# A mixture-of-experts tail: gathering tokens in float32 from X, one more home for expert weights, and two filler products

## The chip, the cores and the metric

The kernel runs on one core of one Trainium2 chip. The metric is the time of one execution on the device in microseconds. TensorE multiplies, VectorE (DVE in the profile), ScalarE (ACT) and GpSimd (POOL) work on elements, and SyncE (SP) issues nearly all DMA transfers, which 16 DMA engines carry out. Weights come from the chip's main memory into on-chip memory of 128 partitions; products are summed in eight banks.

## The reference, cut to what matters

Two transformer blocks over 256 tokens of width 1024. The first has three kinds of attention and a convolutional feed-forward part, the second a gated linear attention, a pooling mixer, and a mixture of experts. The change lies in the last part, which computes:

```python
h2 = rmsnorm_2(x, norm2_g)                       # 256 tokens x 1024
g_p, g_idx = top_k(softmax(h2 @ w_rg + b_rg), 1) # one group of four
e_top, e_idx = top_k(expert logits inside that group, 2)
gate = g_p * softmax(e_top)                      # two weights for each token
# 32 experts; expert e takes the tokens that chose it:
y = (silu(xb @ w_gate[e]) * (xb @ w_up[e])) @ w_down[e]    # 1024 -> 256 -> 1024
x = x + sum over the two experts of gate * y
return rmsnorm_2(x, norm_f_g)
```

All values are float32. The weights of one expert are 3 MB, those of all 32 are 96 MB.

## The kernel before, in words

**Units and homes.** Weights come in units of 128 partitions x 2048 float32 (1 MB, rows of 8 KB). Up to `U_EXP` they run through a ring of six. The 96 units of the experts, three for each (two halves of the gate and up weights, then one of the down weights), go to 22 homes (`DEEP`) in turn: the six of the ring and 16 spaces whose first content is dead by then. `first_homes` lists them in the order of filling; `home_of(n)` gives the home of unit n, `loads_of(n)` how often that home has been loaded. SP issues everything on one queue, in the order of its program (lines 552 to 635). The first 22 units each wait until their home is free (lines 568 to 608): `LAST_1` and `LAST_2`, two homes in the arena, wait until the last unit before the experts is used; `FEATURES` waits for the router's product; `X_SLOT`, the space of X itself, waits until X has been squared, split and added. Each later unit waits until the unit 22 ahead of it has been used (lines 609 to 612). At the end SP loads the row of the final norm into X's space (line 614).

**Order of the work on TensorE** (lines 1240 to 1375): transposes of X, router, expert logits, the residual (X copied into four banks by products with the identity), one filler product (`stay_busy`), ranks of the tokens in their experts, then the gather, the first products of expert 0 and 1, the table of tokens and weights, and a loop over experts. In it come, for each expert: fold, down product, scatter of the expert ahead of it, and up products of the next; every fourth expert, the gather of the next four in two halves.

**Gather.** The tokens of an expert are at most 32 in the first pass (more are treated in a later loop). For four experts at once, the kernel multiplies X with a matrix of zeros and ones, `ONEHOT`. X is taken as two float32r parts: ScalarE copies a high part (`HNH`, lines 1768 and 1775), VectorE subtracts it from X for the low part (`low_part`, L2431 in the profile, four calls), and for each of 8 blocks of 128 features and each half of the tokens, TensorE multiplies the high and the low part with the float32r onehot (L1270): 32 products for a batch. A float32 product appears in the profile as two records, a float32r product as one.

**Around it.** VectorE chooses the experts between the logits and `m_ready` in some 25 dependent small steps, then forms ranks and the onehot, takes the gathered tokens out of the banks, and prepares the operands of the table (`table_in`). ScalarE squares X, and later scales, gates and weights results. VectorE and ScalarE make the weighted results of each expert in the space `YH` ("weighted"), at the place `FFN_FLOAT32` in the arena.

Of the kernel before, what the change touches and what calls it, by code (L numbers as in the profile page):

```python
# [68 lines left out]
DEEP, EARLY, SPARE = 22, 6, 2  # L69
# [14 lines left out]

LEFT = D // 2
# [41 lines left out]
def parts_before(event):  # L127
    return sum(NORM_PARTS[:event])
# [13 lines left out]

class Chain:
# [17 lines left out]
def build(nc, x_in, units_in, const_in, vec_in, rows_in, small_in, bias_in, out):  # L161
# [8 lines left out]
    with ctx:  # L170
# [28 lines left out]
        final_row = X[:, 0, :]  # L199
# [12 lines left out]
        with nc.sbuf_tensor("tokens_low_0", [P, D], f32r) as TOKENS_LOW_0:  # L212
            pass
# [28 lines left out]
        with ExitStack() as space:  # L242
            space.enter_context(nc.sbuf_tensor("ahead_of_parts", [P, PARTS_AT], fp32))
            HNH = space.enter_context(nc.sbuf_tensor("tokens_high", [P, TT, D], f32r))
            TOKENS_LOW_1 = space.enter_context(nc.sbuf_tensor("tokens_low_1", [P, D], f32r))
            ONEHOT = space.enter_context(nc.sbuf_tensor("batch_onehot", [P, TT, BATCH * CH], f32r))
        HNL = (TOKENS_LOW_0, TOKENS_LOW_1)

# [77 lines left out]
        x_space = flat(X[:, :, :])  # L326
# [67 lines left out]
        A.at = TT * D + D + TT * BATCH * CH  # L394
        XB = A.tile(KD, BATCH * CH)
# [13 lines left out]
        kept_loaded = [sem(f"kept_loaded{i}") for i in range(6)]  # L409
# [31 lines left out]
        x_summed = sem("x_summed")  # L441
# [3 lines left out]
        hn_hi, hn_lo = sem("hn_hi"), sem("hn_lo")  # L445
# [19 lines left out]
        TURNED, PARTED, GATED_1, GATED_2, GATED_3, LAST_1, LAST_2, FEATURES, X_SLOT, ROWS = range(RING + EARLY, DEEP)  # L465
        ARENA_HOMES = [0, FFN_FLOAT32 + 2 * KD * S, UNIT, 2 * UNIT, ARENA - UNIT, ARENA - 3 * UNIT, ARENA - 2 * UNIT]
# [4 lines left out]
        slots += [spare_units[:, 0, :], spare_units[:, 1, :], small_units[:, 0, :], small_units[:, 1, :], early_unit[:, :], hn_space,  # L471
                  *(arena[:, a:a + UNIT] for a in ARENA_HOMES), features_unit[:, :], x_space, rows_space]
        slot_loaded += [*spare_loaded, small_loaded, const_loaded, *kept_loaded, x_loaded, second_loaded, ident_loaded, vec_loaded,
                        bias_loaded, rows_loaded]
        loaded_ahead += [0 if s in kept_loaded + spare_loaded else 1 for s in slot_loaded[RING:]]
        assert len(slots) == len(slot_loaded) == DEEP

        def home_of(n):
            return first_homes[(n - U_EXP) % DEEP]
# [4 lines left out]
        LAST_IN_X = max(n for n in range(U_EXP, UNITS) if home_of(n) == X_SLOT)  # L484

        def unit(engine, n, i=0):

            if n < U_EXP:
                engine.wait_ge(unit_loaded[n % RING], 16 * (n // RING + 1) + 16 * i)
                return ring[:, n % RING, :]  # L490
            engine.wait_ge(slot_loaded[home_of(n)], 16 * loads_of(n))
            return slots[home_of(n)]
# [59 lines left out]
        def _(sp):  # L552
            sp.dma_start(X[:, 0, :], x_in[:, 0, :]).then_inc(x_loaded, 16)
# [14 lines left out]
            for k in range(SPARE):  # L568
                at = first_homes[k]
                sp.dma_start(slots[at], units_in[U_EXP + k]).then_inc(slot_loaded[at], 16)  # L570
# [8 lines left out]
            for k in range(SPARE, EARLY):  # L579
# [3 lines left out]
                sp.dma_start(slots[at], units_in[U_EXP + k]).then_inc(slot_loaded[at], 16)  # L583
# [4 lines left out]
            for k in range(EARLY, DEEP):  # L588
# [19 lines left out]
                sp.dma_start(slots[at], units_in[U_EXP + k]).then_inc(slot_loaded[at], 16)  # L608
# [5 lines left out]
            sp.dma_start(final_row, rows_in[:, KEPT:].to_broadcast([P, D])).then_inc(slot_loaded[X_SLOT], 16)  # L614
# [24 lines left out]
        def _(pe):  # L639
# [717 lines left out]
            pe.wait_ge(hn_lo, 2 * TT)  # L1357
# [82 lines left out]
        def _(act):  # L1440
# [326 lines left out]
            act.wait_ge(unit_used, U_EXP)  # L1767
# [1051 lines left out]
```

## Time and profile before

| | us |
|---|---|
| median of 3 runs | 697.87 (697.35 to 697.98) |
| the profiled execution | 697.5 |
| its span | 695.6 |
| TensorE busy | 670.1 (96%) |
| VectorE, ScalarE, GpSimd busy | 355.5, 295.0, 149.1 |
| moved by DMA | 181.46 MB, on average 261 GB/s |

The span runs from the first to the last instruction; the execution is 1.9 us longer. The page cuts the span into 40 slices of 17.4 us. Of busy TensorE it should be known that matmuls are pipelined and their ends modelled, so that 96% says little about whether TensorE sets the time. Waits and chains are inferred from semaphores.

### The profile page before, as it was taken

To read this page: it belongs to the slowest core of one execution; us is meant where nothing else is said; L and a number is where in the kernel's file an instruction comes from. 1 tells how busy PE (TensorE), PEld (TensorE's weight loads), DVE (VectorE), ACT (ScalarE), POOL (GpSimd) and SP (SyncE) were. 2 spreads that over 40 slices of the span, in tenths; PEclk is the share of its full clock that TensorE was granted. 3 is DMA by queue.
4 is the path that set the end of the run, shared out by engine and by line. 5 is a ranking of instruction groups with operands and counts; after the bars stand their busy time and mean duration, and the time that the engine had idled before them with its cause. 6 is when DMAs were issued, how large, how long until landed. Compare 5 with 4: busy or idle time off the path is not lost.

```text
span 695.6 us, 12108 instructions
## 1 busy us (share of the span) xinstructions
PE 670.1 (96%) x4941; PEld 541.2 (78%) x4941; DVE 355.5 (51%) x579; ACT 295.0 (42%) x486; POOL 149.1 (21%) x148
## 2 busy tenths in 40 slices
PE   6999999999999999999999999998899999999984
PEld 5998886999999999977999999985555555555532
DVE  6359544666666666568555564676222323232313
ACT  5244556454444444455574544334113222322223
POOL 0586865033333333322004000000000000000000
PEclk9999999999999999999999999999789999999999
DMA  8961334555555555542443349888699999999994
GB/s 343 423 255 60 123 106 175 212 193 196 191 193 188 181 181 181 182 179 71 175 164 140 139 165 375 329 339 349 239 412 421 420 420 421 421 420 421 420 421 191
DMA packets 25681, 181.46 MB, mean 261 GB/s; under 512 B 2848, under 2 KB 3104, under 8 KB 4128
## 3 DMA queue, kind: packets, MB, share of 16 engines
q1 hardware_dynamic: 25488, 180.69, 66.6%
q8 instruction: 36, 0.59, 0.3%
q10 hardware_dynamic: 144, 0.07, 0.1%
q14 instruction: 13, 0.11, 0.0%
HBM read 179.70 MB, written 1.05 MB: 260 GB/s over the span
## 4 chain that ended last, share of the span: by engine, by line
PE 85%; DMA 4%; DVE 4%; POOL 2%; ACT 2%; issue 1%; SPq 0%; POOLq 0%; ACTq 0%; DVEq 0%
PE psum L682 50%; PE psum L1287 8%; PE psum L1270 4%; PE psum L1311 4%; PE psum L1294 4%; DMA ring<-units_in 4%; PE psum L1303 4%; PE psum L669 1%; PE psum L645 1%; DVE ffn_w_low L531 1%; DVE arena L2256 1%; PE psum L1028 1%; POOL first_odd L1927 1%; DMA const<-const_in 1%; PE psum L721 1%
## 5 line engine op out<-in xcount | busy, mean ns | idle before, releaser
L531 DVE TENSOR_TENSOR ffn_w_low<-ring,ffn_w_high 128x2048 fp32r<-128x2048 f32 x55 | 131.2, 2386 | 111.0 <-ACT ffn_w_high L526 110.8
L526 ACT ACTIVATE ffn_w_high<-ring 128x2048 fp32r<-128x2048 f32 x56 | 107.4, 1918 | 141.2 <-PE psum L682 141.1
L682 PE MATMUL psum<-ht_high,ffn_w_high 128*128 128x256 f32 x552 | 156.8, 284 | 0.8 <-DVE ffn_w_low L531 0.8
L682 PE MATMUL psum<-ht_low,ffn_w_high 128*128 128x256 f32 x552 | 156.2, 283 | 0.0
L682 PE MATMUL psum<-ht_high,ffn_w_low 128*128 128x256 f32 x552 | 156.2, 283 | 0.0
L682 PEld LDWEIGHTS psum<-ht_high,ffn_w_high 128*128 128x128 f32 x552 | 105.9, 192 | 2.5 <-DVE ffn_w_low L531 1.2
L682 PEld LDWEIGHTS psum<-ht_low,ffn_w_high 128*128 128x128 f32 x552 | 105.9, 192 | 0.3
L682 PEld LDWEIGHTS psum<-ht_high,ffn_w_low 128*128 128x128 f32 x552 | 105.9, 192 | 0.0
L2573 DVE SCALAR_TENSOR_TENSOR weighted<-psum,arena,weighted 128x512 fp32r<-128x512 f32 x31 | 23.3, 751 | 70.3 <-ACT weighted L1813 70.3
L1964 POOL TENSOR_TENSOR arena<-arena 128x512 f32<-128x512 f32 x10 | 28.6, 2864 | 119.3 <-ACT arena L1657 96.9
L1791 ACT ACTIVATE arena<-psum,arena 128x512 f32<-128x512 f32 x32 | 22.0, 687 | 61.1 <-PE psum L1287 53.6
L1995 POOL TENSOR_SCALAR ms<-ms 128x1 f32<-128x1 f32 x2 | 0.4, 221 | 209.8 <-ACT arena L1457 209.8
L1311 PEld LDWEIGHTS psum<-weighted,token_onehot 64*128 64x128 f32 x264 | 22.1, 184 | 28.6 <-issue 25.5
L1294 PEld LDWEIGHTS psum<-const,arena 128*128 128x128 f32 x256 | 31.8, 195 | 11.0 <-issue 9.2
L2256 DVE SCALAR_TENSOR_TENSOR arena<-psum,vec,arena 128x255 f32<-128x255 f32 (+1 forms) x88 | 37.3, 476 | 2.7 <-ACT arena L1651 0.6
L1311 PE MATMUL psum<-weighted,token_onehot 64*128 64x512 f32 (+1 forms) x264 | 38.0, 408 | 0.0
L1294 PE MATMUL psum<-const,arena 128*128 128x32 f32 x256 | 35.0, 281 | 1.3 <-ACT arena L1791 1.3
L682 PE MATMUL psum<-ffn_w_high,af_high 128*128 128x512 f32 x88 | 34.5, 393 | 0.5 <-DVE af_low L2297 0.5
L682 PE MATMUL psum<-ffn_w_low,af_high 128*128 128x512 f32 x88 | 34.3, 390 | 0.0
L682 PE MATMUL psum<-ffn_w_high,af_low 128*128 128x512 f32 x88 | 34.2, 389 | 0.0
L1270 PEld LDWEIGHTS psum<-batch_onehot,tokens_high 128*128 128x128 f32 x128 | 25.7, 201 | 9.3 <-issue 8.5
L1270 PE MATMUL psum<-batch_onehot,tokens_high 128*128 128x128 f32 x128 | 31.8, 290 | 0.8 <-DVE batch_onehot L2483 0.8
(398 smaller groups left out, 1296.5 us busy)
## 6 DMA issues: line engine op xcount, KB each, us to landing
ring<-units_in SPq DMA_DIRECT2D x94, 1024.0 KB, 5.0
arena<-units_in SPq DMA_DIRECT2D x29, 1024.0 KB, 22.0
spare_units<-units_in SPq DMA_DIRECT2D x10, 1024.0 KB, 15.6
small_units<-units_in SPq DMA_DIRECT2D x10, 1024.0 KB, 16.9
early_unit<-units_in SPq DMA_DIRECT2D x5, 1024.0 KB, 17.0
HN<-units_in SPq DMA_DIRECT2D x5, 1024.0 KB, 18.7
rows<-units_in SPq DMA_DIRECT2D x4, 1024.0 KB, 17.2
features_unit<-units_in SPq DMA_DIRECT2D x4, 1024.0 KB, 20.9
```

The costliest lines, as they stand in the source:

```text
L526: nc.scalar.activation(parts_slot(n)[0], w, ACT.Copy).then_inc(hi_ready, 1)
L531: nc.vector.tensor_tensor(l, ring[:, n % RING, :], h.bitcast(fp32), SUB).then_inc(lo_ready, 1)
L682: last = mm(o, l[a], r[b], start=start and (a, b) == pairs[0], stop=stop and (a, b) == pairs[-1])
L1270: last = mm(psum[:, bank, n * slots:(n + 1) * slots], part[:, m * P:(m + 1) * P], ONEHOT[:, tt, 0:slots], start=tt == 0 and part is not HN ...
L1287: last = mm(psum[r:r + CH, bank, :], x[:, k, :], w[:, a:a + 2 * D_EXP], start=k < QUADS, stop=k >= KD - QUADS)
L1294: last = mm(psum[:, 1, b * CH:(b + 1) * CH], TS[:, b * P:(b + 1) * P], c_("fold"), start=True, stop=True)
L1303: last = mm(psum[r:r + CH, banks[n], 0:size], AE[:, f, :], w[:, a:a + size], start=True, stop=True)
L1311: last = mm(psum[:, bank + n, columns], W[rows_of, par, tt * P:(tt + 1) * P], YH[rows_of, par, part * 512 + columns.start:part * 512 + col ...
L1791: nc.scalar.activation(TS, psum[:, bank, :], ACT.Copy, scale=roots[:, ds(column, 1)]).then_inc(sums_sb, 1)
L1964: nc.gpsimd.tensor_tensor(AF[:, c % 2], G[:, c % 2], up, MUL).then_inc(af_parts, 1)
L2256: ins = stt(u, psum[:, 2 * (c % 2) + g, f * S:(f + 1) * S - back], vec[:, ds(at + (c0 + (2 - back) * 2 * FF_TILES), 1)], u, MUL, ADD)
L2573: return stt(YH[:, par, 512:], psum[:, 2, :], of[:, ds(column + EXPERTS, 1)], YH[:, par, 0:512].bitcast(fp32), MUL, SUB)
```

## The change

- The gather multiplies X itself with a float32 onehot: 16 float32 products for a batch. `HNH`, `HNL`, `low_part`, the two copies and their semaphores go. `ONEHOT` becomes float32.
- X is no longer a home. The space of the parts becomes a home, `LAST_3`; a further one, `HALVES`, consists of 1024 columns of the former space of the parts and the 1024 of `junk`, and is loaded with two transfers. `DEEP` is 23.
- Expert 0's down unit, `U_BESIDE`, leaves the turn. It is loaded once, behind `LAST_1`, into the space of the weighted results.
- `HALVES` is filled ahead of `FEATURES` and waits for the first of the two squares of X.
- The row of the final norm goes to the home of another unit, and waits for that one's use.
- TensorE gets two more fillers, of 256 columns ahead of the wait for `m_ready` and of 384 behind the rank products. The table moves ahead of expert 1's products.

```diff
-DEEP, EARLY, SPARE = 22, 6, 2
+DEEP, EARLY, SPARE = 23, 6, 2
+U_BESIDE = U_EXP + 4
+class InHalves:
+    def __init__(self, *halves):
+        self.halves = halves
+    def __getitem__(self, at):
+        rows_of, columns = at
+        h, start = divmod(columns.start, UNIT // 2)
+        return self.halves[h][rows_of, start:start + columns.stop - columns.start]
...
-        A.at = TT * D + D + TT * BATCH * CH
-        XB = A.tile(KD, BATCH * CH)
+        A.at = UNIT
+        FIRST_HALF = A.tile(UNIT // 2)
+        ONEHOT, XB = A.tile(TT, BATCH * CH), A.tile(KD, BATCH * CH)
...
-        TURNED, PARTED, GATED_1, GATED_2, GATED_3, LAST_1, LAST_2, FEATURES, X_SLOT, ROWS = range(RING + EARLY, DEEP)
+        TURNED, PARTED, GATED_1, GATED_2, GATED_3, LAST_1, LAST_2, LAST_3, FEATURES, ROWS, HALVES = range(RING + EARLY, DEEP)
+        BESIDE = DEEP
-                        GATED_2, GATED_3, *ring_homes[4:], LAST_1, LAST_2, FEATURES, X_SLOT]
+                        GATED_2, GATED_3, *ring_homes[4:], LAST_1, LAST_2, LAST_3, HALVES, FEATURES]
+        IN_TURN = [n for n in range(U_EXP, UNITS) if n != U_BESIDE]
         def home_of(n):
-            return first_homes[(n - U_EXP) % DEEP]
+            return BESIDE if n == U_BESIDE else first_homes[IN_TURN.index(n) % DEEP]
+        LAST_AHEAD_OF_ROW = next(n for n in range(UNITS - DEEP, UNITS) if RING + EARLY <= home_of(n) < HALVES)
...
+            def load(n):
+                at = home_of(n)
+                if at == HALVES:
+                    for h, space in enumerate(slots[at].halves):
+                        sp.dma_start(space, units_in[n][:, h * UNIT // 2:(h + 1) * UNIT // 2]).then_inc(slot_loaded[at], 16)
+                else:
+                    sp.dma_start(slots[at], units_in[n]).then_inc(slot_loaded[at], 16)
...
-                if at == X_SLOT:
-                    sp.wait_ge(squares_summed, parts_before(FINAL))
-                    sp.wait_ge(hn_lo, 2 * TT)
-                    sp.wait_ge(x_summed, 1)
-                sp.dma_start(slots[at], units_in[U_EXP + k]).then_inc(slot_loaded[at], 16)
-            for n in range(U_EXP + DEEP, UNITS):
-                at = home_of(n)
-                sp.wait_ge(unit_used, n - DEEP + 1)
-                sp.dma_start(slots[at], units_in[n]).then_inc(slot_loaded[at], 16)
-            sp.wait_ge(unit_used, LAST_IN_X + 1)
+                if at == HALVES:
+                    sp.wait_ge(squares_summed, parts_before(FINAL) - 1)
+                load(IN_TURN[k])
+                if at == LAST_1:
+                    load(U_BESIDE)
+            for k in range(DEEP, len(IN_TURN)):
+                sp.wait_ge(unit_used, IN_TURN[k - DEEP] + 1)
+                load(IN_TURN[k])
+            sp.wait_ge(unit_used, LAST_AHEAD_OF_ROW + 1)
...
             residual(0)
-            residual(1).then_inc(x_summed, 1)
+            residual(1)
             stay_busy(1, 2, c_("iota"))
+            stay_busy(1, 2, c_("iota"), 256)
             pe.wait_ge(m_ready, 1)
...
             last.then_inc(rank_done, 1)
+            stay_busy(1, 2, c_("iota"), 384)
...
                     for tt in range(TT):
-                        for part in (HNH[:, tt, :], HNL[tt]):
-                            last = mm(psum[:, bank, n * slots:(n + 1) * slots], part[:, m * P:(m + 1) * P],
-                                      ONEHOT[:, tt, 0:slots], start=tt == 0 and part is not HNL[tt],
-                                      stop=tt == TT - 1 and part is HNL[tt])
+                        last = mm(psum[:, bank, n * slots:(n + 1) * slots], X[:, tt, m * P:(m + 1) * P],
+                                  ONEHOT[:, tt, 0:slots], start=tt == 0, stop=tt == TT - 1)
...
-            pe.wait_ge(hn_lo, 2 * TT)
...
+            pe.wait_ge(table_in, 1)
+            table(TABLE_BANK, 0).then_inc(table_done, 1)
             for g in range(2):
                 expert_up(tokens_for(1), unit(pe, gate_of(1) + g), range(g * HALF_K, (g + 1) * HALF_K)
                           ).then_inc(unit_used, 1)
-            pe.wait_ge(table_in, 1)
-            table(TABLE_BANK, 0).then_inc(table_done, 1)
...
-            copy(HNH[:, 0, :], X[:, 0, :]).then_inc(hn_hi, 1)
...
-            copy(HNH[:, 1, :], X[:, 1, :]).then_inc(hn_hi, 1)
...
-            for half in range(2):
-                low_part(0, half)
...
-            low_part(1, 0)
...
-            low_part(1, 1)
```

## Rows read from the trace of the kernel before

**Rows 1.** The page's slices: GB/s moved in each 40th of the span.
```profile
GB/s 343 423 255 60 123 106 175 212 193 196 191 193 188 181 181 181 182 179 71 175 164 140 139 165 375 329 339 349 239 412 421 420 420 421 421 420 421 420 421 191
```

**Rows 2.** The chain that ended last, its end: start us, us, what.
```profile
658.87 26.32 DMA ring<-units_in
...
685.24 1.07 PE psum L1303 x16
```

**Rows 3.** Stretches: each engine's busy us, granted clock (PEclk), DMA share, GB/s.
```profile
484.30:497.00 12.70, 11.05 (x66) 7.22 (x69) 6.04 (x24) 2.31 (x5) 0.00 (x0) 0.73 0.35 121
497.00:682.00 185.00, 179.03 (x1446) 97.03 (x1440) 50.49 (x117) 49.31 (x93) 0.00 (x0) 0.98 1.01 418
```

**Rows 4.** The chain in the experts' loop, from one batch's gather to the next.
```profile
606.88 1.93 PE psum L1270 x16
...
613.73 1.85 PE psum L1287 x16
...
630.12 1.93 PE psum L1270 x16
```

**Rows 5.** Timeline of TensorE near the end: start, us, instructions, idle before.
```profile
667.86 1.07 PE L1303 MATMUL psum<-spare_units,arena 128*32 128x512 f32 x8 [0.97 <-DMA spare_units<-units_in]
```

**Rows 6.** Stretches again, short ones around the DMA engines' idle time.
```profile
484.80:486.30 1.50, 0.71 (x5) 0.63 (x5) 1.34 (x5) 0.64 (x2) 0.00 (x0) 1.00 0.08 33
486.30:487.20 0.90, 0.12 (x2) 0.10 (x1) 0.81 (x5) 0.89 (x2) 0.00 (x0) 1.00 0.00 0
487.20:488.40 1.20, 1.20 (x12) 1.20 (x12) 0.32 (x4) 0.16 (x1) 0.00 (x0) 1.00 0.79 184
...
490.50:495.60 5.10, 5.10 (x27) 2.82 (x30) 2.21 (x7) 0.62 (x2) 0.00 (x0) 0.50 0.00 0
```

**Rows 7.** Timeline of SP's queue: start, us, line, transfers issued.
```profile
475.40 1.05 SPq L608 DMA_DIRECT2D arena<-units_in  x2
479.21 0.33 SPq L608 DMA_DIRECT2D features_unit<-units_in  x1
486.29 0.33 SPq L608 DMA_DIRECT2D X<-units_in  x1
494.65 1.75 SPq L612 DMA_DIRECT2D spare_units<-units_in  x2
...
507.06 0.33 SPq L612 DMA_DIRECT2D HN<-units_in  x1
```

**Rows 8.** Timeline of ScalarE: the first square of X, its sum.
```profile
474.89 0.18 ACT L1457 ACTIVATION_READ_ACCUMULATOR junk<-X 128x1 f32 x1
```

**Rows 9.** The chain around the choice of experts and the first gather.
```profile
479.81 0.19 DVE tokens_low L2431
...
487.10 5.62 PE psum L1270 x32
```

**Rows 10.** Timeline of VectorE: the last operand of the table.
```profile
494.68 0.35 DVE L2521 TENSOR_TENSOR arena<-arena 128x192 f32<-128x192 f32 x1
```

**Rows 11.** Timeline of TensorE: float32 products (a product is two records).
```profile
120.13 3.84 PE L669 MATMUL psum<-HN,X 128*128 128x128 f32 x32 [0.61 <-DVE HN L2029]
...
479.71 0.64 PE L1250 MATMUL psum<-const,arena 128*128 128x36 f32 x4 [0.54 <-DVE arena L2439]
480.18 3.68 PE L1237 MATMUL psum<-X,const 128*128 128x512 f32 x8
```

**Rows 12.** Stretches by granted clock (PEclk, third number from the end).
```profile
485.00:488.90 3.90, 2.53 (x21) 2.44 (x21) 2.27 (x12) 1.69 (x3) 0.00 (x0) 0.98 0.40 124
488.90:495.20 6.30, 6.30 (x30) 4.23 (x34) 3.14 (x10) 0.62 (x2) 0.00 (x0) 0.50 0.23 95
...
502.30:509.00 6.70, 6.70 (x36) 2.77 (x32) 1.57 (x4) 1.14 (x3) 0.00 (x0) 0.51 1.01 421
```

**Rows 13.** Stretches with rows of 4 KB: the start and the last row.
```profile
2.00:4.00 2.00, 0.00 (x0) 0.00 (x0) 1.57 (x3) 0.44 (x1) 0.00 (x0) 1.00 0.87 230
...
685.20:686.10 0.90, 0.86 (x16) 0.42 (x16) 0.83 (x2) 0.14 (x2) 0.00 (x0) 1.00 0.10 41
```

More of the change, by code:

```diff
@@ L211, in build @@
         sb("features", [P, KD * S])
-        with nc.sbuf_tensor("tokens_low_0", [P, D], f32r) as TOKENS_LOW_0:
-            pass
         junk = sb("junk", [P, D])
@@ L241, in build @@
             YH = space.enter_context(nc.sbuf_tensor("weighted", [P, 2, D], f32r))
[L242 to L247, printed above, removed]
         MIX_AT, TOKENS_AT = 6216, 17032
@@ L408, in build @@
         unit_loaded = [sem(f"unit_loaded{i}") for i in range(RING)]
-        kept_loaded = [sem(f"kept_loaded{i}") for i in range(6)]
+        kept_loaded = [sem(f"kept_loaded{i}") for i in range(8)]
         spare_loaded = [sem(f"spare_loaded{i}") for i in range(SPARE)]
@@ L473, in build @@
-        slot_loaded += [*spare_loaded, small_loaded, const_loaded, *kept_loaded, x_loaded, second_loaded, ident_loaded, vec_loaded,
-                        bias_loaded, rows_loaded]
+                  *(arena[:, a:a + UNIT] for a in ARENA_HOMES), features_unit[:, :], rows_space,
+                  InHalves(FIRST_HALF, junk[:, :]), arena[:, FFN_FLOAT32:FFN_FLOAT32 + UNIT]]
+        slot_loaded += [*spare_loaded, small_loaded, const_loaded, *kept_loaded[0:6], x_loaded, second_loaded, ident_loaded,
+                        vec_loaded, bias_loaded, rows_loaded, *kept_loaded[6:8]]
@@ L475, in build, with arrived @@
         loaded_ahead += [0 if s in kept_loaded + spare_loaded else 1 for s in slot_loaded[RING:]]
-        assert len(slots) == len(slot_loaded) == DEEP
+        assert len(slots) == len(slot_loaded) == DEEP + 1
+        IN_TURN = [n for n in range(U_EXP, UNITS) if n != U_BESIDE]
         def home_of(n):
-            return first_homes[(n - U_EXP) % DEEP]
+            return BESIDE if n == U_BESIDE else first_homes[IN_TURN.index(n) % DEEP]
         def loads_of(n):
             return loaded_ahead[home_of(n)] + sum(home_of(m) == home_of(n) for m in range(U_EXP, n + 1))
-        LAST_IN_X = max(n for n in range(U_EXP, UNITS) if home_of(n) == X_SLOT)
+        def arrived(n):
+            return (32 if home_of(n) == HALVES else 16) * loads_of(n)
@@ L486, in unit @@
+        LAST_AHEAD_OF_ROW = next(n for n in range(UNITS - DEEP, UNITS) if RING + EARLY <= home_of(n) < HALVES)
+        ROW_SLOT = home_of(LAST_AHEAD_OF_ROW)
+        final_row = slots[ROW_SLOT][:, 0:D]
         def unit(engine, n, i=0):
@@ L490, in unit @@
                 return ring[:, n % RING, :]
-            engine.wait_ge(slot_loaded[home_of(n)], 16 * loads_of(n))
+            engine.wait_ge(slot_loaded[home_of(n)], arrived(n))
             return slots[home_of(n)]
@@ L603, in _ @@
                     sp.wait_ge(lg_done, 1)
-                if at == X_SLOT:
-                    sp.wait_ge(squares_summed, parts_before(FINAL))
-                    sp.wait_ge(hn_lo, 2 * TT)
-                    sp.wait_ge(x_summed, 1)
-                sp.dma_start(slots[at], units_in[U_EXP + k]).then_inc(slot_loaded[at], 16)
-            for n in range(U_EXP + DEEP, UNITS):
-                at = home_of(n)
-                sp.wait_ge(unit_used, n - DEEP + 1)
-                sp.dma_start(slots[at], units_in[n]).then_inc(slot_loaded[at], 16)
-            sp.wait_ge(unit_used, LAST_IN_X + 1)
-            sp.dma_start(final_row, rows_in[:, KEPT:].to_broadcast([P, D])).then_inc(slot_loaded[X_SLOT], 16)
+                if at == HALVES:
+                    sp.wait_ge(squares_summed, parts_before(FINAL) - 1)
+                load(IN_TURN[k])
+                if at == LAST_1:
+                    load(U_BESIDE)
+            for k in range(DEEP, len(IN_TURN)):
+                sp.wait_ge(unit_used, IN_TURN[k - DEEP] + 1)
+                load(IN_TURN[k])
+            sp.wait_ge(unit_used, LAST_AHEAD_OF_ROW + 1)
+            sp.dma_start(final_row, rows_in[:, KEPT:].to_broadcast([P, D])).then_inc(slot_loaded[ROW_SLOT], 16)
             sp.wait_ge(total_ready, 1)
@@ L2426, in _ @@
             take_transposes(4, None)
-            def low_part(tt, half):
-                dve.wait_ge(hn_hi, tt + 1)
-                at = slice(half * LEFT, (half + 1) * LEFT)
-                tt_op(HNL[tt][:, at], X[:, tt, at], HNH[:, tt, at].bitcast(fp32), SUB).then_inc(hn_lo, 1)
-            for half in range(2):
-                low_part(0, half)
             V_.tensor_copy(rank_terms[:, 0:2 * P], const[:, CC["ones"].start:CC["stri"].stop])
@@ L2669, in _ @@
             dve.wait_ge(y_done, 2)
-            dve.wait_ge(slot_loaded[X_SLOT], 16 * (loads_of(LAST_IN_X) + 1))
+            dve.wait_ge(slot_loaded[ROW_SLOT], arrived(LAST_AHEAD_OF_ROW) + 16)
             tt_op(HN[:, 1, 0:LEFT], psum[:, 6, :], final_row[:, 0:LEFT], MUL).then_inc(last_rows, 1)
```

10 lines of the change are left out of this document (1 added, 9 removed).

## The prediction

> **What bounds the kernel now.** I read the slices of the page first. From slice 29 on the DMA engines move 420 GB/s and hold it to the end, while the slice ahead moves 239 [rows 1]. Whether they or TensorE set the end, the slices do not say; the chain of waits does. The last unit of expert weights is issued at 658.87, lands 26.32 us later, and the last expert's products start right behind it [rows 2]; then only fixed work of 10 us follows, to 695.6. The 26 us are not one transfer but a queue: at 418 GB/s [rows 3] a unit of 1.0486 MB takes 2.51 us, so some ten units are in it. TensorE alone would be done sooner. The first half of a batch's gather comes again after four experts, twelve units, and there that is 23.24 us [rows 4], 1.94 us a unit against 2.51. It first waits for a unit at 666.9 [rows 5]. So the end is a date of the DMA engines: the bytes that remain at a steady rate, plus every microsecond in which they had nothing to move.
>
> The third view is a table of their share. Between 497 and 682 no time is lost; between 484.3 and 497.0 only 121 GB/s are moved, which as a mean over the 16 engines loses 12.7 x (1 - 121/418) = 9.0 us [rows 3]. In finer steps [rows 6]: to 486.3 about one engine in sixteen still moves something (share 0.08; 1/16 is 0.06); from 486.3 to 487.2 nothing moves; then comes a restart, 1.2 us at 184 GB/s; from 490.5 to 495.6 nothing moves, and then a second restart.
>
> SP's queue says why [rows 7]. At 475.4 it issues the last two arena homes, at 479.21 the features' home, and at 486.29 the home in X, which waited for VectorE's last low part of X. The next issue waits until expert 0's first unit is used, at 494.65.
>
> **The change part by part.** *Homes.* Today four units are issued between 475.4 and the first release. After the change there are six: LAST_1, the unit beside (expert 0's down unit), LAST_2, LAST_3, HALVES, FEATURES. LAST_3 and the unit beside need only what LAST_1 waits for; HALVES waits for the first square of X, done at 475.1 [rows 8]. Six issues ahead of FEATURES (HALVES has two) at 0.53 us each (two took 1.05, [rows 7]) end at 478.6, when little over a unit has moved, so the queue does not run dry. Three units keep the engines until 484.3 today; six keep them until 484.3 + 3 x 2.51 = 491.8, the lagging one until 486.3 + 7.5 = 493.8.
>
> *First release.* What is late next is the first use of expert 0's unit. VectorE's chain to the onehot stays, but for the low part that stands in it at 479.81 with 0.19 us [rows 9]. In its place come the expert logits on TensorE, which start at 479.71 and are 0.64 us long [rows 11]: a gain between 0 and 0.2 us, I take 0.1. The other low parts and ScalarE's two copies of X lie beside the transposes, the router and the residual products, and count as nothing; if that cover were gone they would cost nothing either, since they are removed.
>
> *Fillers.* Eight records of 512 columns in float32 took 3.68 us, two of which make one product [rows 11]. So 256 columns cost 0.46 us and 384 cost 0.69. The one stands ahead of the wait for the chosen experts, the other ahead of the wait for the onehot; from 485.0 to 488.9 TensorE was idle for 3.90 - 2.53 = 1.37 us [rows 12], all of it in these two waits, since the gather behind them is dense. 1.15 us of fillers in 1.4 us of waits count as nothing at full clock. At half clock the second would take 1.4 us and hold the gather up by 0.6.
>
> *Gather.* 32 products in float32r become 16 in float32, each of which shows as two records. The trace has this form: products of X with a diagonal of the same size, 32 records in 3.84 us, 0.120 each [rows 11]. The float32r ones take 0.121 at full clock (16 in 1.93 us, [rows 4]). So the loop gains nothing. The first gather, though, took 5.62 us [rows 9], since the granted clock fell to 0.50 at 488.9 (1.2 of the two levels 1.2 and 2.4 GHz), behind those two waits [rows 12]. The fillers close most of them, and I take the clock as held: gather from 487.0 to 490.8, then half of an expert's products (1.85 us for both halves, [rows 4]) to 491.7. Today that is 494.65. The bounds are 491.7 and, if the clock falls as today, 494.2 (rival a).
>
> Data flow 1.0 us behind the issue (494.65 to 495.6, [rows 6, 7]), so at 492.7: 0.9 us after the mean engine runs dry and 1.1 us before the lagging one does.
>
> *Table ahead of expert 1.* The second release follows at 492.6. The table waits for VectorE, which had its operands ready at 495.03, 2.3 us behind the end of the gather [rows 9, 10], so at 493.1; what queues behind this wait are expert 1's products alone. The table's eight records take about 1.1 us (0.12 to 0.14 each, as any of the [rows 11] in float32), and the third and fourth release come at 495.2 and 496.1. The engines need the third by 496.7 (492.7 + 2 x 2.51 - 1.0) and the fifth by 501.7. The unit beside frees no home when it is used, so the fifth release is expert 2's. It comes at most one expert of the loop, 5.81 us, behind the fourth, at 501.9: level with the need at worst. From there a release each 1.94 us meets a need each 2.51.
>
> *Halves.* One home of 23 is loaded as two transfers in rows of 4 KB, four times in the 95 units of the turn. Lower bound nothing: from 685.2 only the last row is left, 4 KB for each partition, and a busy engine then moves at 41/0.10 = 410, as at 418/1.01 with 8 KB [rows 3, 13]. Upper bound: in the first microseconds, where X arrives in such rows, 230/0.87 = 264 [rows 13], 1.5 us more for each load, 6 us in all. That stretch also holds smaller rows and the first start; the tail is the same queue in the same state. I take nothing.
>
> The Trainium skill speaks against the halves ("DMA: Bandwidth & Descriptors", section "Bandwidth", with the fit in "Anatomy of one DMA"): it gives a transfer a fixed 2.0 us beside its bytes, and asks for 1 MiB or more. By that, as an estimate from the page, four cut loads cost 8 us and the time would be 699. The trace differs: whole units follow one another in 2.51 us, where the page's fit has 4.4.
>
> *Final row.* It gets another home and no longer waits for a late unit, but stays behind the last unit in the same queue: nothing.
>
> **Sum.** A unit is there when its last part is, so the lagging engine counts. It lost 0.9 + 5.1 us with nothing to move and 1.2 x (1 - 184/418) = 0.67 us in a restart, twice: 7.3 us [rows 6]; the mean engine lost 9.0. I leave 0.3 us for gaps: a gain of 7.0 us. The profiled execution took 697.5 us with a span of 695.6, so it becomes 690.5. The median of the runs, 697.87, is 0.4 above it; I forecast 690.8. TensorE has to follow. Expert 2 comes some 5 us earlier (its first unit was used at 507.06 by SP's issue, [rows 7]), the last units 7; TensorE makes up 0.57 us on each unit and today has caught up 18 us, seven units, ahead of the last landing [rows 2, 5], so 2 us are made up in four.
>
> **Rivals.** (a) *The clock falls at the gather all the same.* For: it does today, and again at 502.3 [rows 12]. Against: the idle waits ahead of it are nearly gone. Then some 15 records run at 0.12 and 17 at 0.21 (30 in 6.3 us, [rows 12]): the gather ends at 492.4, half an expert at half clock is 1.85 us, the release is at 494.2, and the lagging engine waits from 493.8 to 495.2 and restarts: gain 7.3 - 2.0 = 5.3, 692.5.
> (b) *Every engine gains, not only the lagging one.* For: the engine left over at 485 need not be the one that ends last. Then 9.0 - 0.9, 689.7.
> (c) *Releases behind the fourth come late,* since the table waits longer or the clock falls in expert 1. For: the fall at 502.3. At half clock a release each 3.9 us meets the need each 2.5; over two or three units that costs 3 us: 693.8.
> (d) *The other side: the halves hold the queue.* Place: every load of HALVES from 477 on. Price: at the start's rate 1.5 us each, 696.8; the gain is gone from 1.75 us each; at half the rate, 2.5 us, it is 690.8 + 10 = 700.8. For: the rows of the start. Against: those of the tail.
> (e) *The change does not do what it says:* SP stands in order, so if the wait of HALVES or FEATURES came late, the two more homes would wait too, and only the earlier release is left: 3 us, 694.8. Against: both events are dated, 475.1 and 479.2.
>
> **How the numbers follow.** Forecast (690.0 to 691.6) 0.50; (a) 0.20; (b) 0.08; (c) 0.09; (e) 0.03; (d) 0.10, of which 0.01 is still faster, 0.03 without difference, 0.06 slower. The range takes in the forecast, (a), (b) and (c): 689.2 to 694.2. What a measurement of this kernel can tell from no change is 0.2%, 1.4 us: "same" is 696.5 to 699.3. Faster 0.50 + 0.20 + 0.08 + 0.09 + 0.03 + 0.01 = 0.91, same 0.03, slower 0.06.
>
> **What would show it.** Right: a DMA share of 1.0 from 484 to 491 and a gap under 1 us behind it; the first release on SP at 491 to 492; the granted clock 1.00 from 485 to 495 and the first gather in 3.8 us; the last unit landing near 678 with the same 10 us behind it. Wrong: a gap at 493 to 495 (a), a lower rate while a HALVES load is moved (d), or a chain whose end runs through TensorE and not through a transfer.

## The result, and the profile after

The changed kernel takes 688.57 us (median; 687.72 to 689.11), the kernel before 697.92 beside it (697.35 to 698.98): a ratio of 0.9862, interval 0.9847 to 0.9878, a gain of 9.35 us. The forecast was 690.8, the range 689.2 to 694.2. The sign was as forecast; the time is 2.2 us shorter than forecast and lies 0.6 us below the range. The profiled execution took 688.96 us with a span of 687.1, that of before 697.5: between these two the gain is 8.5.

The end is what it was. The chain that ended last in the changed kernel (start, us, what), with the first gather and the table in it:
```profile
479.79 0.65 PE psum L1267 x4
...
487.13 3.85 PE psum L1288 x32
...
493.34 1.13 PE psum L1336 x8
...
651.69 25.13 DMA small_units<-units_in
676.86 1.07 PE psum L1320 x16
```
The last unit waits 25 us in the queue, lands at 676.8, and 10.3 us of fixed work follow, as in [rows 2], where it landed at 685.2. The gather takes 3.85 us in place of 5.62 [rows 9]. The expert logits in VectorE's place gave nothing one can see: the next step of that chain starts at 480.46, before it was 480.42.

The page's slices of GB/s, which answer to [rows 1]:
```profile
GB/s 341 425 268 61 124 74 173 245 184 184 184 186 186 186 184 183 186 180 56 184 185 139 142 186 272 362 303 403 372 422 421 418 421 422 421 418 421 421 419 202
```
The slice of 239 ahead of the steady stretch is now 372. By stretches, in the changed kernel (the columns of [rows 3]: the stretch and its length, the busy us of TensorE, of its weight loads, of VectorE, ScalarE and GpSimd, then the granted clock, the DMA share and GB/s):
```profile
476.30:520.00 43.70, 41.37 (x312) 23.70 (x314) 18.85 (x69) 13.11 (x25) 0.54 (x1) 1.00 0.99 393
484.30:497.00 12.70, 11.75 (x90) 7.36 (x88) 5.77 (x25) 3.00 (x6) 0.00 (x0) 1.00 0.97 365
497.00:505.00 8.00, 7.27 (x63) 3.80 (x66) 2.71 (x7) 3.09 (x6) 0.00 (x0) 1.00 1.00 402
505.00:515.00 10.00, 10.00 (x84) 6.17 (x87) 3.10 (x7) 1.82 (x4) 0.00 (x0) 1.00 1.02 428
520.00:660.00 140.00, 140.00 (x1160) 77.00 (x1152) 40.24 (x92) 38.35 (x72) 0.00 (x0) 1.00 1.01 420
485.00:488.90 3.90, 3.47 (x24) 2.63 (x23) 1.69 (x11) 1.69 (x3) 0.00 (x0) 1.00 0.98 359
488.90:495.20 6.30, 5.78 (x51) 3.57 (x53) 3.46 (x12) 0.90 (x3) 0.00 (x0) 1.00 0.93 351
487.10:489.20 2.10, 2.07 (x18) 2.08 (x19) 0.45 (x5) 0.28 (x2) 0.00 (x0) 1.00 0.97 298
492.50:495.20 2.70, 2.18 (x20) 1.25 (x20) 1.10 (x5) 0.28 (x1) 0.00 (x0) 1.00 0.79 264
```
and the same in the kernel before, where no row of the prediction has them:
```profile
476.30:520.00 43.70, 39.36 (x246) 22.72 (x245) 18.31 (x65) 12.40 (x23) 0.54 (x1) 0.84 0.81 316
497.00:505.00 8.00, 5.98 (x40) 3.91 (x32) 1.56 (x5) 2.18 (x4) 0.00 (x0) 0.84 0.99 384
505.00:515.00 10.00, 10.00 (x68) 4.24 (x67) 1.79 (x5) 2.51 (x5) 0.00 (x0) 0.79 1.00 401
```
Between 484.3 and 497.0 the engines now move 365 GB/s where they moved 121 [rows 3]. The granted clock is 1.00 in every stretch, the higher of the two levels, where it was 0.50 between 488.9 and 495.2 [rows 12]. And the rate between 497 and 515 was below the steady 420 before the change, with a DMA share of 0.99 and 1.00 beside it: the share did not show that loss, the rate does.

SP's queue in the changed kernel (start, us, line, transfers), which answers to [rows 7]:
```profile
475.49 2.29 SPq L570 DMA_DIRECT2D arena<-units_in  x4
477.82 0.51 SPq L568 DMA_DIRECT2D arena<-units_in  x1
478.37 0.44 SPq L568 DMA_DIRECT2D junk<-units_in  x1
479.30 0.33 SPq L570 DMA_DIRECT2D features_unit<-units_in  x1
492.02 1.19 SPq L570 DMA_DIRECT2D spare_units<-units_in  x2
495.52 1.19 SPq L570 DMA_DIRECT2D small_units<-units_in  x2
501.19 0.33 SPq L570 DMA_DIRECT2D early_unit<-units_in  x1
```
Six units are issued from 475.49 to 479.6, with one wait of 0.5 us ahead of the last; the first release comes at 492.02, the third at 495.52, the fifth at 501.19. TensorE around these waits (start, us, instructions, idle before):
```profile
485.62 0.73 PE L1279 MATMUL psum<-rank_terms 128*128 128x32 f32 x5 [0.40 <-DVE rank_terms L2482]
486.20 0.89 PE L662 MATMUL psum<-const 128*128 128x384 f32 x2
487.13 3.84 PE L1288 MATMUL psum<-arena,X 128*128 128x128 f32 x32
490.89 1.92 PE L1304 MATMUL psum<-spare_units,arena 128*32 128x512 f32 x16
493.34 1.13 PE L1336 MATMUL psum<-arena 128*128 128x96 f32 x8 [0.52 <-DVE arena L2525]
```
The fillers are gone into the two waits: 0.40 us are left of the first, ahead of the products that rank the tokens, nothing is left of the second, ahead of the gather, and TensorE is idle for 0.52 us ahead of the table.

### The profile page after: what moved, and what is told of

The parts are those of the page before. It is cut to its first block, busy times and chain, and to the rows that moved or that the text cites. A ratio compares the mean times of both kernels' runs of the same rounds, so it can differ in the third digit from the quotient of the medians.

```text
span 687.1 us, 12112 instructions
## 1 busy us (share of the span) xinstructions
PE 665.5 (97%) x4945; PEld 538.9 (78%) x4945; DVE 353.2 (51%) x575; ACT 293.1 (43%) x484; POOL 149.1 (22%) x148
## 3 DMA queue, kind: packets, MB, share of 16 engines
HBM read 179.70 MB, written 1.05 MB: 263 GB/s over the span
## 4 chain that ended last, share of the span: by engine, by line
PE 86%; DMA 4%; DVE 4%; POOL 2%; issue 1%; ACT 1%; SPq 0%; POOLq 0%; DVEq 0%; ACTq 0%
PE psum L699 51%; PE psum L1304 7%; PE psum L1328 4%; PE psum L1288 4%; PE psum L1311 4%; PE psum L1320 4%; DMA small_units<-units_in 4%; PE psum L662 1%; PE psum L686 1%; DVE ffn_w_low L542 1%; DVE arena L2269 1%; PE psum L1045 1%; POOL first_odd L1940 1%; DMA const<-const_in 1%; PE psum L738 1%
## 5 line engine op out<-in xcount | busy, mean ns | idle before, releaser
L1288 PEld LDWEIGHTS psum<-arena,X 128*128 128x128 f32 x256 | 29.7, 191 | 9.1 <-issue 8.4
L1899 POOL TENSOR_TENSOR rstd<-ms,neghalf 128x1 f32<-128x1 f32 (+3 forms) x9 | 7.0, 772 | 118.2 <-DVE ms L2034 105.9
```

What stands on the lines that cost most here:

```text
L1288: last = mm(psum[:, bank, n * slots:(n + 1) * slots], X[:, tt, m * P:(m + 1) * P], ONEHOT[:, tt, 0:slots], start=tt == 0, stop=tt == TT - 1)
```

## Experiments

Two theories of the size of the gain. **Theory A:** what counts is the mean over the 16 engines, that is, the bytes not moved against the steady 420 GB/s, over the whole stretch from LAST_1's issue until the rate is steady. **Theory B:** what counts is the engine that ends last, that is, the time in which no engine moves anything, as the prediction had it. For A, "lost" below is 43.7 x (1 - GB/s / 420) in the row 476.30:520.00: 10.8 us before, 2.8 after.

**The change again, beside its parts.** No edit.

> The changed kernel once more, as the measure for the runs beside it. From its first runs: 688.6 us, 9.3 us under the kernel before. Theory A (what counts is the time that the DMA engines lost as a mean over all 16: 9.0 us between 484.3 and 497.0, and a little more up to 515) asks for 8.2 to 8.7 between two profiled executions. Theory B (the engine that lags sets the end; it lost 7.3) asks for 7.0.

688.53 us (688.37 to 689.59), ratio 0.9872 (0.9858 to 0.9886). The stretch from 476.3 to 520:
```profile
476.30:520.00 43.70, 41.36 (x310) 23.47 (x312) 19.07 (x69) 13.15 (x25) 0.55 (x1) 1.00 0.99 400
```
2.1 us lost, 8.7 fewer than before; between the profiled executions the gain is 9.0. The gain is repeated, and it is nearer to A's 8.2 to 8.7 than to B's 7.0.

**The unit beside left out.**
```diff
-U_BESIDE = U_EXP + 4
+U_BESIDE = -1
...
-                if at == LAST_1:
-                    load(U_BESIDE)
```

> The changed kernel without the unit beside: expert 0's down unit goes through the 23 homes in turn, so five units instead of six stand between 475.5 and the first release. Theory A: the queue runs dry one unit earlier, at 490.0 instead of 492.5, the release stays at 492.0, so 2.5 us more: 691.1. Theory B: the lagging engine runs dry 1.8 us behind the others, so only 0.7 to 1.2 us more: 689.3 to 689.8.

690.69 us (690.50 to 690.84): the unit is worth 2.16. How the stream ends ahead of the first release at 491.83:
```profile
476.30:520.00 43.70, 41.37 (x310) 23.51 (x312) 19.05 (x69) 13.12 (x25) 0.54 (x1) 1.00 0.93 378
...
489.20:490.00 0.80, 0.80 (x10) 0.80 (x9) 0.77 (x3) 0.03 (x1) 0.00 (x0) 1.00 0.45 184
490.00:490.80 0.80, 0.80 (x11) 0.68 (x14) 0.05 (x1) 0.60 (x2) 0.00 (x0) 1.00 0.08 31
490.80:492.40 1.60, 1.60 (x16) 0.34 (x16) 1.52 (x6) 0.00 (x0) 0.00 (x0) 1.00 0.00 0
```
Lost are 4.4 us, 2.3 more than in the repeat with the unit, as A has it. But the last engine lags the others by only some 1.3 us here, and nothing moves for 1.8 (in the table below), so B with a restart comes near as well: this run alone tells them apart weakly.

**The fillers left out.**
```diff
-            stay_busy(1, 2, c_("iota"), 256)
...
-            stay_busy(1, 2, c_("iota"), 384)
```

> The changed kernel without its two fillers. If they hold the clock: it falls to 0.50 in the first gather, the first release comes at about 494.2 instead of 492.0, and the time is 2.2 us more by theory A, 690.8 (1 us or less by theory B, 689.6). If the float32 gather holds the clock by itself, nothing changes: 688.6.

690.88 us, with runs from 688.42 to 692.50. The profiled execution (690.96):
```profile
484.30:497.00 12.70, 10.60 (x77) 7.74 (x77) 5.33 (x23) 3.00 (x6) 0.00 (x0) 0.87 0.85 321
497.00:505.00 8.00, 7.27 (x49) 3.11 (x48) 1.97 (x6) 1.85 (x5) 0.00 (x0) 0.79 1.05 420
```
The clock falls behind the open waits, the first release slips to 493.14, and 2.35 us are gone. It was rival (a), and the fillers keep it out. The fastest of the six runs, 688.42, had a mean granted clock of 0.998 over its whole time, the profiled one 0.992: the clock does not fall alike each time.

**The kernel before with the unit beside.**
```diff
+U_BESIDE = U_EXP + 4
...
-                  *(arena[:, a:a + UNIT] for a in ARENA_HOMES), features_unit[:, :], x_space, rows_space]
+                  *(arena[:, a:a + UNIT] for a in ARENA_HOMES), features_unit[:, :], x_space, rows_space, arena[:, FFN_FLOAT32:FFN_FLOAT32 + UNIT]]
...
+                if at == LAST_1:
+                    sp.dma_start(slots[DEEP], units_in[U_BESIDE]).then_inc(slot_loaded[DEEP], 16)
```

> The kernel before with one part alone: expert 0's down unit waits in the space of the results, issued behind LAST_1; everything else as before. 2.5 us of the time in which nothing moved (490.5 to 495.6) are filled: 695.4 by both theories. If it is hidden anyway or the wait only moves: 697.9.

696.88 us, ratio 0.9991 (0.9968 to 1.0014): no difference that can be told, where about 2.5 us were expected. The stretches, and below them SP's fifth release:
```profile
476.30:520.00 43.70, 39.37 (x247) 22.63 (x245) 18.53 (x65) 12.27 (x22) 0.54 (x1) 0.84 0.84 328
484.30:497.00 12.70, 11.05 (x70) 7.10 (x69) 5.83 (x23) 2.32 (x5) 0.00 (x0) 0.73 0.54 199
497.00:505.00 8.00, 5.99 (x44) 4.11 (x40) 1.56 (x5) 2.36 (x5) 0.00 (x0) 0.83 0.97 367
505.00:515.00 10.00, 10.00 (x69) 4.29 (x61) 1.79 (x5) 2.34 (x5) 0.00 (x0) 0.79 0.94 360
```
```profile
506.71 0.33 SPq L617 DMA_DIRECT2D early_unit<-units_in  x1
```
The unit fills 2.4 us of the gap (199 GB/s against 121). Between 497 and 515 some 1.3 of them are lost again (367 and 360 against 384 and 401): the unit beside gives no home back, so the fifth release waits for expert 2, on a granted clock of 0.8, and comes at 506.71, where the kernel before has it at 503.32, when expert 0's down unit is used. The unit pays only where the releases behind it come early. The profiled execution is 1.1 us faster than that of before, as the row of 476.3 to 520 has it (9.6 us lost in place of 10.8); the twelve runs spread from 691.4 to 700.5, too wide to show so little. The 691.4 is the one run of the twelve with a granted clock of 0.996; the others have 0.984 to 0.989.

**Every later unit in halves.**
```diff
-            return (32 if home_of(n) == HALVES else 16) * loads_of(n)
+            return 32 * loads_of(n) - 16 * loaded_ahead[home_of(n)]
...
-                    sp.dma_start(slots[at], units_in[n]).then_inc(slot_loaded[at], 16)
+                    for h in range(2):
+                        part = slice(h * UNIT // 2, (h + 1) * UNIT // 2)
+                        sp.dma_start(slots[at][:, part], units_in[n][:, part]).then_inc(slot_loaded[at], 16)
```

> The changed kernel with every unit of the experts loaded as two transfers of 512 KB in rows of 4 KB, not only HALVES: 92 more cut loads. If rows of 4 KB and a second transfer are free in a full queue: within 1 us of the changed kernel, 688.6. If each cut load costs what the first HALVES load seemed to (the rate fell to about 290 GB/s between 487.1 and 489.2, 0.65 us): some 70 of them lie in the full queue, 45 us more. At the rate of the kernel's start (1.5 us each): over 100 us more. By the fixed 2.0 us a transfer of the Trainium skill (DMA: Bandwidth & Descriptors): about 140 us more.

694.66 us, 6.1 more than the changed kernel, for some 70 more cut loads: 0.087 us each. The steady stretch:
```profile
520.00:660.00 140.00, 138.79 (x1140) 76.26 (x1132) 39.62 (x89) 38.25 (x71) 0.00 (x0) 1.00 1.03 409
```
409 GB/s in place of 420 is 1.0486/0.409 - 1.0486/0.420 = 0.07 us for each unit, about the same. The change's four cut loads cost, as an estimate from these rows, some 0.35 us: not nothing, but far from rival (d)'s 1.5 us for each of them.

The Trainium skill ("DMA: Bandwidth & Descriptors", "Anatomy of one DMA") has a fixed 2.0 us for each transfer. It gives them for transfers that GpSimd issues, and counts most of them as the time until the end is confirmed. In this full queue, which SyncE issues, they do not show as lost rate: the second transfer of a unit added under 0.1 us.

**The kernel before with the fillers.** The diff is against the kernel before.
```diff
+            stay_busy(1, 2, c_("iota"), 256)
...
+            stay_busy(1, 2, c_("iota"), 384)
```

> The kernel before with the two fillers alone. If they hold the clock through the float32r gather: gather in 3.9 us instead of 5.6, first release near 491.9 instead of 494.65, 2.7 us less lost: 695.2 by both theories. If the clock falls all the same: 697.9.

694.48 us, ratio 0.9953 (0.9936 to 0.9969), 3.8 us faster:
```profile
484.30:497.00 12.70, 10.94 (x87) 7.25 (x86) 5.84 (x24) 3.00 (x6) 0.00 (x0) 0.99 0.62 222
497.00:505.00 8.00, 7.27 (x36) 3.35 (x39) 2.06 (x6) 1.71 (x4) 0.00 (x0) 0.50 1.01 424
505.00:515.00 10.00, 10.00 (x76) 4.95 (x68) 1.96 (x5) 2.97 (x5) 0.00 (x0) 0.90 0.99 366
```
The clock holds through the gather and the first release comes at 491.35 in place of 494.65, but then the clock falls to 0.50 and 505 to 515 runs at 366 GB/s. The next two waits of TensorE:
```profile
496.21 1.47 PE L1296 MATMUL psum<-const,arena 128*128 128x32 f32 x8 [1.28 <-ACT arena L1793]
498.41 1.94 PE L1305 MATMUL psum<-early_unit,arena 128*32 128x512 f32 x8 [0.73 <-DVE arena L2586]
```
The fall stands between the two: the granted clock is 0.99 from 496.0 to 496.7 and 0.50 from 496.7 to 499, so only the wait of 1.28 us is ahead of it. The fillers move the fall; they do not end it.

**The table behind expert 1, in the changed kernel.**
```diff
-            pe.wait_ge(table_in, 1)
-            table(TABLE_BANK, 0).then_inc(table_done, 1)
             for g in range(2):
...
+            pe.wait_ge(table_in, 1)
+            table(TABLE_BANK, 0).then_inc(table_done, 1)
```

> The changed kernel with the table's products behind expert 1's again. Third and fourth release 1.6 us earlier (493.9, 494.8), but the fold of expert 0 waits for the table and its sums, so the fifth release comes about 2 us later, near 503 to 504, when the queue has run dry or nearly. Theory A: 0 to 1.5 us more, 689.3. If only the first releases count: 0.5 us less, 688.1.

691.74 us (688.78 to 693.21), 3 us slower than with the table ahead:
```profile
497.00:505.00 8.00, 7.27 (x35) 3.01 (x38) 2.06 (x6) 1.72 (x4) 0.00 (x0) 0.57 0.90 358
```
The same finding from the other side: the third release is earlier (493.12 against 495.52), but the wait for ScalarE is there again, 1.29 us ahead of 496.26, where the table's turn ahead of expert 1 had left none; the clock falls to 0.57 on the mean, and the fifth release comes at 503.75, 2.6 us later. What the order of the table takes away is that wait.

**The kernel before with fillers and the table ahead.** The fillers as above, and the table moved the other way:
```diff
+            pe.wait_ge(table_in, 1)
+            table(TABLE_BANK, 0).then_inc(table_done, 1)
             for g in range(2):
...
-            pe.wait_ge(table_in, 1)
-            table(TABLE_BANK, 0).then_inc(table_done, 1)
```

> The kernel before with the two fillers and the table ahead of expert 1's products, homes and gather as before. With the fillers alone the granted clock held through the gather and fell to 0.50 between 497 and 505, behind the idle time around the table, and the fifth release came late. If the order of the table is what holds the clock there: granted clock 1.00 to 520, no loss after 497, 2 us less than with the fillers alone: 692.5. If it is only the fillers that count: 694.5.

692.80 us (692.46 to 693.08), ratio 0.9926 (0.9913 to 0.9940), as expected:
```profile
476.30:520.00 43.70, 41.31 (x313) 23.16 (x311) 20.91 (x73) 14.12 (x27) 0.54 (x1) 1.00 0.88 356
...
497.00:505.00 8.00, 7.67 (x64) 3.76 (x68) 2.89 (x8) 2.94 (x6) 0.00 (x0) 1.00 1.01 423
```
The clock is 1.00 throughout, and nothing is lost from 497 to 505. Of the gain, 5.4 us need no space at all: they come from the fillers and the order of TensorE's work. The runs of the unchanged kernel say the same: of the 28 that stand beside the fillers' run, two took 692.95 and 693.33, at granted clocks of 0.995 and 0.992, and the other 26 took 696.1 to 699.3, at 0.984 to 0.988.

**The change with 22 homes and no unit beside.** The edit of the unit beside above, and:
```diff
-DEEP, EARLY, SPARE = 23, 6, 2
+DEEP, EARLY, SPARE = 22, 6, 2
...
-                        GATED_2, GATED_3, *ring_homes[4:], LAST_1, LAST_2, LAST_3, HALVES, FEATURES]
+                        GATED_2, GATED_3, *ring_homes[4:], LAST_1, LAST_2, HALVES, FEATURES]
```

> The changed kernel with 22 homes and no unit beside: LAST_3 goes too, so four units stand between 475.3 and the first release, as in the kernel before, but HALVES comes at 477 where X came at 486. By the mean loss of the engines: dry one more unit earlier than without the unit beside, 2.5 us more than that kernel's 690.7, 693.2. If the homes counted for less than the order of the work: under 692.

693.29 us (692.95 to 693.37), ratio 0.9932 (0.9918 to 0.9945), as expected:
```profile
476.30:520.00 43.70, 41.37 (x310) 23.45 (x311) 19.06 (x69) 13.12 (x25) 0.54 (x1) 1.00 0.88 352
```
So the steps from before to after are: order of work 698.2 to 692.8; float32 gather, the cut home and what goes with them 692.8 to 693.3; LAST_3 693.3 to 690.7; the unit beside 690.7 to 688.5 (the kernel before had 698.2 beside the runs of 692.8 and 693.3, and 698.0 beside those of 690.7 and 688.5). Each of the two units is worth 2.6 and 2.2, about the 2.5 us for which the engines move it. These prices hold for this order of the steps: on the kernel before, the unit beside gave nothing that can be told.

**Expert 0's first half ahead of the last two gathered blocks.** An earlier first release, in the changed kernel:
```diff
-            for bank, features in FIRST_GROUPS:
+            for bank, features in FIRST_GROUPS[0:2]:
                 gather(bank, features).then_inc(gathered, 1)
...
+            for bank, features in FIRST_GROUPS[2:]:
+                gather(bank, features).then_inc(gathered, 1)
```

> The changed kernel with the first half of expert 0's products ahead of the last two of the eight gathered blocks. The first release comes 0.9 us earlier, near 491.1, and the gap in the DMA share at 492.5 to 493.5 with its restart closes. Theory A: 0.9 to 1.2 us less, 687.5. Theory B (the lagging engine was not dry there): no change, 688.6. A third way: the second half, the table and the later releases are each 0.9 us later and the gap moves to the third release: no change.

690.76 us, with runs from 688.09 to 693.04, where 687.5 was expected. The one profiled execution is the 688.09:
```profile
490.44 3.04 SPq L570 DMA_DIRECT2D spare_units<-units_in  x2
496.02 1.19 SPq L570 DMA_DIRECT2D small_units<-units_in  x2
```
The first release is 1.6 us earlier, the third 0.5 later: the gap moves behind the second unit. Why other runs take up to 693 no trace here shows; their granted clocks point to falls of the clock: the three runs above 691 have 0.993 and 0.994, the three below 0.995 to 0.999.

**The table between the halves of expert 1, and both.**
```diff
-            for g in range(2):
-                expert_up(tokens_for(1), unit(pe, gate_of(1) + g), range(g * HALF_K, (g + 1) * HALF_K)
-                          ).then_inc(unit_used, 1)
+            expert_up(tokens_for(1), unit(pe, gate_of(1)), range(HALF_K)).then_inc(unit_used, 1)
+            pe.wait_ge(table_in, 1)
+            table(TABLE_BANK, 0).then_inc(table_done, 1)
+            expert_up(tokens_for(1), unit(pe, gate_of(1) + 1), range(HALF_K, KD)).then_inc(unit_used, 1)
```
The other kernel adds the edit before it.

> The changed kernel with the table's products between the two halves of expert 1's. The half fills the 0.5 us in which TensorE waits for VectorE's operands; the third release comes 1.5 us earlier (493.7), the fourth 0.5 us earlier, the fold too. The share lost between 493.5 and 497 (some 0.5 us) closes and no idle time is added: 0.3 to 0.8 us less, 687.9. If the engines are fed in time anyway: 688.5.

> Both: the first half of expert 0's products ahead of the last gathered blocks, and the table between the halves of expert 1's. First release 1.4 us earlier, third 1.5 us earlier than with the early use alone: 1.0 us less than the changed kernel, 687.5. If the early use spread its times from 688 to 693 because the waits behind it let the clock fall: a spread again, unless the half ahead of the table closes them.

690.28 us (688.78 to 690.56) and 689.78 (689.61 to 690.84); no version was faster than the change. In the first the third release is 2.5 us earlier (493.06), and the clock falls:
```profile
497.00:505.00 8.00, 7.87 (x40) 2.94 (x40) 1.81 (x5) 1.78 (x4) 0.00 (x0) 0.57 0.93 363
```
It is 0.84 on the mean from 496 to 498 and 0.50 from 498 to 500. Ahead of this fall TensorE has only these waits behind the gather:
```profile
495.35 1.05 PE L1311 MATMUL psum<-const,arena 128*128 128x32 f32 x8 [0.29 <-ACT arena L1803]
497.13 1.76 PE L1320 MATMUL psum<-arena 128*32 128x512 f32 x8 [0.73 <-DVE arena L2587]
```
In the second kernel the clock stays at 1.00, though the same two waits of 0.29 and 0.73 us stand there (ahead of 496.59 and 498.37) and one of 0.56 us more; but 3.3 us are lost against 2.1 to 2.8 in the change. So the lengths of the waits alone do not say whether the clock falls.

**All runs together.** For each profiled execution: its time; LAST_1's issue; GB/s from 476.3 to 520; A's loss; and what is left of the time when LAST_1's issue and the loss are taken off. The last two columns are B's: the time between 483 and 519 in which no engine moved anything (steps of 0.3 us, share under 0.02), and what is left by it.
```
                      time    LAST_1  GB/s  A lost  A left   B idle  B left
before                697.50  475.40   316   10.8   211.3     6.0    216.1
after                 688.96  475.49   393    2.8   210.7     0.0    213.5
the change again      688.50  475.27   400    2.1   211.2     0.0    213.2
no unit beside        690.84  475.29   378    4.4   211.2     1.8    213.8
no fillers            690.96  474.97   376    4.6   211.4     0.3    215.7
before, beside        696.44  475.18   328    9.6   211.7     4.2    217.1
before, fillers       693.82  474.81   343    8.0   211.0     3.9    215.1
table behind          691.57  474.86   371    5.1   211.6     0.0    216.7
early use             688.09  474.76   397    2.4   210.9     0.0    213.3
before, dense         692.46  474.75   356    6.7   211.0     3.3    214.4
22 homes              693.23  475.25   352    7.1   210.9     3.9    214.1
table between         690.56  474.82   380    4.2   211.6     0.0    215.7
both                  689.88  475.06   388    3.3   211.5     0.0    214.8
```
What is left by A is 210.7 to 211.7 in thirteen executions whose times differ by 9.4 us. By B it spreads over 3.9 us. Kernels without any time in which nothing moved differ by 3.5 us (688.09 and 691.57), and no price for a restart can bridge that. B falls. (Every unit in halves is not in the list: its rate behind 520 is another.) That A's last column is so even is in part bookkeeping, since what was not moved before 520 is moved behind it at the same 420 GB/s. What it tests is that nothing else was lost: that the rate held to the end, and that in no kernel one engine ended later than the mean by more than in another.

## Why the prediction was right in kind and wrong in size

**Right.** That the end is a date of the DMA engines, with the same fixed work behind it. Six units issued before the queue could run dry; the mean engine was dry at 492.5 (said: 491.8); first release 492.02 (491.7); gather 3.85 us (3.8) with the clock held; table's operands ready at 493.3 (493.1); third release 495.52 (495.2); fifth 501.19 (501.9 at most); fillers free (the two waits were 0.88 and 0.78 us, 1.66 in all and not 1.37, since the first began ahead of 485.0). Rivals (a), (c), (d) and (e) did not happen, and the run without fillers and the one with the table behind show that (a) and (c) were near. That the last units land earlier than [rows 2], by 8.4 us where 7 were said, and that TensorE follows, is as said in kind, too.

**The step that failed** is in the sum: "A unit is there when its last part is, so the lagging engine counts." The table above shows the mean. Nothing shows that the engine left over at 485 [rows 6] was the one that ended last: before the first release of the changed kernel no such engine lags by 2 us any more. The share is 1.03 from 492.1 to 492.4 and 0.33 from 492.7 to 493.0, when new data come. Rival (b) had the right mechanism and a chance of 0.08. In size this error was partly hidden. From 484.3 to 497.0 the mean loss went from 9.0 to 12.7 x (1 - 365/420) = 1.7 us: a gain of 7.4, beside a forecast of 7.3 less 0.3. I had one term too small by 1.7 and the gap that remains (0.3 allowed) too small by 1.4; that the two nearly cancel is luck. Of that gap, 1.0 us lies between 492.5 and 495.2, around the restart behind the first release, and 0.6 between 487.1 and 489.2, where HALVES is first moved, at 298 GB/s.

**The second step that failed** is "Between 497 and 682 no time is lost". From 497 to 505 the loss was 8 x (1 - 384/420) = 0.7 us, from 505 to 515 10 x (1 - 401/420) = 0.5. In the kernel before:
```profile
498.00:500.00 2.00, 0.77 (x7) 0.61 (x6) 0.32 (x2) 0.69 (x1) 0.00 (x0) 1.00 0.96 307
```
```profile
503.32 0.33 SPq L612 DMA_DIRECT2D early_unit<-units_in  x1
```
Most of the first loss, 0.5 us, lies between 498 and 500, at a granted clock of 1.00 and ahead of the fifth release at 503.32, behind the restart; what makes it stays open. The second lies behind the sixth release, expert 2's at 507.06, which came late on the lower clock [rows 7, 12]; that this is its cause is likely but not shown. A mean of 418 over 185 us [rows 3] hid both. After the change this part loses 0.3 and wins 0.2 back (402 and 428): 1.0 us of gain that no term of the sum had.

**The balance** between the profiled executions, forecast 7.0, measured 8.5: 7.4 + 1.0, less 0.4 in the rest of the 43.7 us (10.8 - 2.8 = 8.0 in all), less 0.1 since LAST_1 is later, and 0.6 by which what is left differs (211.3 and 210.7), within its spread. The remaining 0.8 to the measured 9.35 is how the profiled executions lie to their medians: before 0.4 below it, after 0.4 above it. So of the 2.3 us by which the gain was missed, 0.9 stand in stretches of the traces; the other 1.4 are scatter that no step of the sum can be charged with.

**The halves** I took as nothing; by the run with every unit in halves they cost about 0.35 us. The dip at the first of them is no fixed price of the cut: without the unit beside, the same load is moved from 484.0 to 487.5 at 420 GB/s.

## What to carry to other kernels

Where the end is a date of a stream, price a change by the bytes that it did not move: the deficit of the mean rate over the whole stretch until the rate is steady, in windows short enough that a loss of 1 us shows, not by the time in which nothing moves, nor by the last engine, nor by the DMA share. A buffer that holds a unit but gives no home back fills a hole now and opens one later, unless the releases behind it come earlier as well. Work that is moved into TensorE's waits can be worth more than the space one fights for, here 5.4 of some 9.4 us, but only if the clock then holds to the end of the stretch: with one wait of 1.28 us left open, the fall only moved behind it. Measure it, since waits as short as 0.29 and 0.73 us stood once ahead of a fall and once not.

## What was not expected of the hardware

- Cutting a 1.05 MB load in two costs 0.07 to 0.09 us in a full queue (409 against 420 GB/s over 140 us).
- The first of the change's cut loads moved at 298 GB/s (487.1 to 489.2), the same load at 420 in the run without the unit beside (484.0 to 487.5) and at 279 in that with 22 homes (482.0 to 484.5). Why, stays open.
- The granted clock fell to 0.50 behind a wait of 1.28 us (fillers on the kernel before) and held at 1.00 with waits of 0.40, 0.52 and 0.73 us (the change). With 0.29 and 0.73 us it fell in one kernel (the table between) and held in another (both).
- Kernels in which the clock falls in the profiled execution or in single runs spread over 2 to 5 us from run to run (688.4 to 692.5 without the fillers, 688.1 to 693.0 with the early use), while the eight runs of the change itself spread over 1.9 (687.7 to 689.6).
